# Stick-breaking attention: items taken two by two in the order of work

## The reference

```python
def stick_breaking_block(q_blk, k_ctx, v_ctx, q0):
    ...
    z = jnp.einsum('bthd,bshd->bhts', q_blk, k_ctx) * (SB_HEAD_DIM ** -0.5)
    before = jnp.arange(s_len)[None, :] < (q0 + jnp.arange(tq))[:, None]
    log_keep = jnp.where(before, jax.nn.log_sigmoid(-z), 0.0)
    csum = jnp.cumsum(log_keep, axis=-1)
    weights = jnp.where(before, jnp.exp(jax.nn.log_sigmoid(z) + csum[..., -1:] - csum), 0.0)
    return jnp.einsum('bhts,bshd->bthd', weights, v_ctx)

def stick_breaking_layer(h, norm_w, w_in, w_out):
    u = rmsnorm(h, norm_w)
    q, k, v, g = jnp.split(u @ w_in, 4, axis=-1)
    ...
    o = (o * jax.nn.silu(g.astype(jnp.float32))).astype(h.dtype)
    return h + o @ w_out
```

## Time and profile before

| | |
|---|---|
| runs, us | 3859.55, 3864.09, 3866.41 (median 3864.09) |
| span of the profiled execution | 3862.8 us |
| PE busy | 3735.6 us (97%) |
| DVE, ACT, POOL busy | 2372.8, 1653.3, 1689.3 us |

### The profile page before, as it was taken

The page is one execution under the profiler, slowest core; times in us unless marked ns, Lnnn a source line. Parts: engine busy times, 40 slices in busy tenths (PEclk is TensorE's granted clock), DMA queues, the critical chain, the costliest instruction groups (busy, mean ns, idle before and its releaser), DMA issues.

```text
span 3862.8 us, 50418 instructions
## 1 busy us (share of the span) xinstructions
PE 3735.6 (97%) x19892; PEld 3040.4 (79%) x19892; DVE 2372.8 (61%) x3104; ACT 1653.3 (43%) x2799; POOL 1689.3 (44%) x1108
## 2 busy tenths in 40 slices
PE   8999999999999899999999899999999999999998
PEld 6888887666655466888887799999878988888877
DVE  7667685633555548667684767554577156666664
ACT  5333444322222335333444553411572356666663
POOL 4555554344444535555553243422532233443464
PEclk9999999999999999999999999999999999999999
DMA  3234574200000121234574011221121300000024
GB/s 121 96 109 150 194 247 135 88 23 28 22 17 17 50 85 57 96 113 153 202 238 133 29 44 44 65 89 61 48 69 56 134 32 23 30 25 28 28 69 140
DMA packets 143917, 327.30 MB, mean 85 GB/s; under 512 B 16896, under 2 KB 20512, under 8 KB 143296
## 3 DMA queue, kind: packets, MB, share of 16 engines
q1 hardware_dynamic: 132368, 281.80, 21.9%
q0 software_dynamic: 8752, 39.65, 2.7%
q10 hardware_dynamic: 2560, 2.61, 0.2%
HBM read 252.37 MB, written 71.63 MB: 84 GB/s over the span
## 4 chain that ended last, share of the span: by engine, by line
PE 78%; DVE 13%; ACT 5%; POOL 2%; issue 2%; DMA 0%; ACTq 0%; DVEq 0%; SPq 0%; POOLq 0%
PE ps L958 6%; PE ps L959 6%; PE ps L960 6%; PE ps L414 5%; PE ps L415 5%; PE ps L416 5%; PE ps L4316 4%; PE ps L978 3%; PE ps L977 3%; PE ps L976 3%; PE ps L4248 2%; PE ps L4250 2%; PE ps L4249 2%; PE ps L2059 2%; PE ps L4300 2%; PE ps L2061 2%
## 5 line engine op out<-in xcount | busy, mean ns | idle before, releaser
L388 POOL TENSOR_TENSOR wlo<-raw,whi 128x1024 fp32r<-128x1024 f32 x154 | 377.1, 2453 | 483.9 <-ACT whi L379 483.7
L414 PE MATMUL ps<-xh,whi 128*128 128x352 f32 (+1 forms) x1400 | 473.3, 338 | 7.4 <-DVE xl L671 2.7
L415 PE MATMUL ps<-xh,wlo 128*128 128x352 f32 (+1 forms) x1400 | 450.6, 322 | 0.0
L416 PE MATMUL ps<-xl,whi 128*128 128x352 f32 (+1 forms) x1400 | 450.1, 321 | 0.0
L861 POOL TENSOR_TENSOR fwl<-fpb,fwh 128x512 fp32r<-128x512 f32 x204 | 302.3, 1491 | 267.1 <-ACT fwh L851 266.8
L861 POOL TENSOR_TENSOR fwl<-fpa,fwh 128x512 fp32r<-128x512 f32 x202 | 293.6, 1462 | 278.9 <-ACT fwh L851 278.8
L4621 POOL TENSOR_TENSOR ospl<-osp,osph 128x672 fp32r<-128x672 f32 (+4 forms) x144 | 190.9, 1326 | 357.9 <-ACT osph L4442 356.8
L414 PEld LDWEIGHTS ps<-xh,whi 128*128 128x128 f32 x1400 | 265.4, 190 | 19.2 <-POOL wlo L388 6.6
L415 PEld LDWEIGHTS ps<-xh,wlo 128*128 128x128 f32 x1400 | 264.3, 189 | 8.0 <-issue 2.2
L416 PEld LDWEIGHTS ps<-xl,whi 128*128 128x128 f32 x1400 | 264.1, 189 | 0.0
L958 PE MATMUL ps<-fxh,fwh 128*128 128x512 f32 x640 | 249.3, 390 | 1.3 <-ACT u L1036 1.3
(11 more groups left out here) (505 smaller groups left out, 9708.4 us busy)
## 6 DMA issues: line engine op xcount, KB each, us to landing
raw<-in_w_dram SPq DMA_DIRECT2D x154, 512.0 KB, 3.7
hs_scratch<-u SPq DMA_DIRECT2D x176, 256.0 KB, 2.4
u<-hs_scratch SPq DMA_DIRECT2D x118, 256.0 KB, 2.9
fpa<-in_fg_dram SPq DMA_DIRECT2D x88, 256.0 KB, 3.8
fpb<-in_fg_dram SPq DMA_DIRECT2D x88, 256.0 KB, 3.8
fpa<-in_fd_dram SPq DMA_DIRECT2D x88, 256.0 KB, 3.5
fpb<-in_fd_dram SPq DMA_DIRECT2D x88, 256.0 KB, 3.7
acc<-hs_scratch SPq DMA_DIRECT2D x80, 256.0 KB, 2.7
```

Of the source, the lines that this page charges most:

```text
L388: pool.x.tensor_tensor(K.wlo[n % 3][:, :], K.raw[n % 2][:, :], K.whi[n % 3][:, :], ALU.subtract).then_inc(*S.up("w_lo", n))
L414: pe.x.matmul(out, wh, xh, start=k == 0, stop=False)
L415: pe.x.matmul(out, wl, xh, start=False, stop=False)
L416: last = pe.x.matmul(out, wh, xl, start=False, stop=k == K - 1)
```

## The change

Items are taken in steps of two, (0, 1), (2, 3) and so on; nine steps for each head pair. In a step with items a' and b' the list has, in this order: if the first of the two items from two steps ago was the last of its chunk, its mix; z of a' and z of b'; a turn; the remaining mixes of two steps ago; then, once for a' and once for b': its copy, the sums of one of the previous step's items (a, then b), four fill steps, that item's rest, and the soft of a' (or b'). The splitting of weights by POOL (lo unit) and the issue of gate loads come at the end of a step. The places of the last pair's extra work are set anew, and its fill begins after eight items, where it began after six. No instruction's shape and no buffer is altered.

```diff
--- before.py
+++ after.py
@@ -4131,28 +4131,26 @@
 
 def _odd_places():
 
-    out, pipe = [], [None] * 5
-
-    def step(it, lo_unit):
-        pipe.insert(0, it)
-        if pipe[1]:
-            out.append(("soft", pipe[1]))
+    out, pipe = [], [(), (), ()]
+
+    def step(items, lo_unit):
+        pipe.insert(0, items)
+        first = int(len(pipe[2]) > 0 and pipe[2][0][3] == 0)
+        out.extend(("mix", it) for it in pipe[2][:first])
+        out.extend(("z", it) for it in items)
+        for it in items:
+            if it[1] < 7 and it[0] % PER_T in (12, 14, 16):
+                out.append(("turn", (it[1] + 1, it[0] % PER_T // 2 - 6)))
+        out.extend(("mix", it) for it in pipe[2][first:])
+        for m in range(2):
+            out.extend(("copy", it) for it in items[m:m + 1])
+            out.extend(("sums", it) for it in pipe[1][m:m + 1])
+            out.append(("fill", 4))
+            out.extend(("rest", it) for it in pipe[1][m:m + 1] if it[3])
+            out.extend(("soft", it) for it in items[m:m + 1])
         if lo_unit is not None:
             out.append(("lo unit", lo_unit))
-        if it is not None:
-            out.append(("z", it))
-            if it[1] < 7 and it[0] % PER_T in (12, 14, 16):
-                out.append(("turn", (it[1] + 1, it[0] % PER_T // 2 - 6)))
-            out.append(("copy", it))
-        if pipe[3]:
-            out.append(("mix", pipe[3]))
-        if pipe[2]:
-            out.append(("sums", pipe[2]))
-        out.append(("fill", 4))
-        if pipe[2] and pipe[2][3]:
-            out.append(("rest", pipe[2]))
-        if pipe[4] and not pipe[4][3]:
-            out.append(("gate", 3 * pipe[4][1] + pipe[4][2] + 2))
+        out.extend(("gate", 3 * it[1] + it[2] + 2) for it in pipe[2] if not it[3])
         pipe.pop()
 
     unit = UNIT_AT["Q.8"] + 3
@@ -4160,35 +4158,34 @@
         if t < 7:
             out.append(("begin", t + 1))
         lo_unit = None
-        for m, it in enumerate(ODD[PER_T * t:PER_T * (t + 1)], 1):
-            step(it, lo_unit)
+        for m in range(0, PER_T, 2):
+            step(ODD[PER_T * t + m:PER_T * t + m + 2], lo_unit)
             lo_unit = None
-            if t < 7 and m % 6 == 2:
+            if t < 7 and m % 6 == 0:
                 unit += 1
                 lo_unit = unit
                 out.append(("hi unit", unit))
             if t == 7:
-                out.extend(LAST_PAIR.get(m, ()))
+                out.extend(LAST_PAIR[m // 2])
         if t < 7:
             out.append(("fill", 1000))
-    for _ in range(4):
-        step(None, None)
+    for _ in range(2):
+        step((), None)
     out.extend([("fill", 1000), ("part", (2, 4)), ("rows", (2, 0)), ("rows", (2, 1))])
     return out
 
 
-LAST_PAIR = {m: [("part", (0, m - 1))] for m in (1, 2, 3, 4)}
-LAST_PAIR[5] = [("part", (1, 0))]
-LAST_PAIR[6] = [("part", (0, 4)), ("begin", 8)]
-LAST_PAIR[4].append(("rows", (0, 0)))
-LAST_PAIR[7] = [("rows", (0, 1)), ("part", (1, 1))]
-LAST_PAIR[8] = [("part", (1, 2))]
-LAST_PAIR[9] = [("rows", (1, 0)), ("part", (1, 3))]
-LAST_PAIR[10] = [("part", (2, 0))]
-LAST_PAIR[11] = [("part", (2, 1))]
-LAST_PAIR[12] = [("part", (1, 4))]
-LAST_PAIR[13] = [("rows", (1, 1)), ("part", (2, 2))]
-LAST_PAIR[14] = [("part", (2, 3))]
+LAST_PAIR = {
+    0: [("part", (0, 0)), ("part", (0, 1))],
+    1: [("part", (0, 2)), ("part", (0, 3)), ("rows", (0, 0))],
+    2: [("part", (1, 0))],
+    3: [("part", (0, 4)), ("begin", 8), ("rows", (0, 1)), ("part", (1, 1))],
+    4: [("part", (1, 2))],
+    5: [("rows", (1, 0)), ("part", (1, 3)), ("part", (2, 0))],
+    6: [("part", (1, 4)), ("part", (2, 1))],
+    7: [("rows", (1, 1)), ("part", (2, 2))],
+    8: [("part", (2, 3))],
+}
 ODD_PLACES = _odd_places()
```

## The result

| | before | changed |
|---|---|---|
| median of four runs each, us | 3864.6 | 3898.98 |
| range of the runs | 3859.55 to 3866.41 | 3892.84 to 3901.18 |
| span of the profiled execution | 3862.8 | 3891.0 |

The changed kernel is slower: the ratio is 1.0086, with a 95% interval from 1.0071 to 1.0101. (The kernel before has one run more here than in the table ahead of the prediction.) The profiled execution was the quickest of its four (3892.84); the others had spans of 3896.4 to 3899.3 at a mean clock of 0.983, against 0.985 in the profiled one.

The account below looks back on a forecast made before the run. PE, busy 97% of the span, was taken as the bound. Per pair -2.8 + 4.2 + 3.0 - 0.6 = +3.8 us, 26.6 in seven, and -2.5 for the last pair gave span 3886.9, time 3887.5; 8-in-10 range 3858 to 3907.

Parts of the forecast that it names:

- The saving: PE's matmuls in each head pair: fewer changes of array shape save 2.8 us per pair, bounds 2.4 and 3.3.
- The first wait: z of a step's second item waits for the max of the previous step's second item: 4.2 us per pair.
- The second wait: Second item's min waits for POOL ahead of turn's copy, copy and add, so PE waits: 3.0 us per pair net.
- The overlap: Pairs 0 to 6: a PE that comes later waits less at four places, so 0.6 us per pair comes off.
- The last pair: Last head pair, with eight items without fill in place of six: taken as -2.5 us, from -6 to +6.
- A: Rival: faster, only the saved shape switches count and the waits of z and min don't bind; 3842 us, chance 0.20.
- B: Rival: no change, z waits as computed but the min doesn't hold back copy and add; 3866.5 us, chance 0.15.
- C: Rival: slower still, both waits lengthen each other, each step loses 0.2 us more; 3904 us, chance 0.15.

Follow-up runs that it names:

- e3_both: Changed kernel with the max of each step's second item ahead of the second fill and its min behind the first item's add; 3840.07 us, ratio 0.9931.
- e8_ctrl: Kernel before, items single, with the max of every item ahead of the fill; 3863.32 us, ratio 1.0000.
- e2_min: Changed kernel with min, exp and ln of each step's second item moved behind the add of the previous step's first item; 3869.01 us, ratio 1.0009.
- e1: Changed kernel with DVE taking the max of each step's second item ahead of the second fill, and so of the low part; 3854.94 us, ratio 0.9969.
- e6: Kernel before with z of the odd item drawn up behind z of the even one, all else single; 3882.58 us, ratio 1.0050.
- e4_last: Changed kernel with the last pair's fill beginning after six items, as before, in place of eight; 3887.89 us, ratio 1.0056.
- e7_all: Changed kernel with second item's max ahead of the second fill, its min behind the add, and last pair's fill from item 6; 3835.38 us, ratio 0.9925.

## Why the prediction was right, and where its terms were off

The direction was right, and the time of 3887.5 lies 11.5 us under the median, in the range. Against its own execution the sum gave a span of 3886.9 where 3891.0 came. That is two errors that partly cancel: pairs 0 to 6 gave +23.0 at the last gate multiply of pair 6 (3690.31 before, 3713.27 now) where the sum had +26.6, and the tail gave +5.3 where the sum had -2.5. Together they are 28.3, the whole difference of the spans (28.2). That the sum missed the span by 4.1 only is thus in part luck. The other 7.4 of the 11.5 us lie outside the sum. 6.1 are those by which the median is above the profiled execution. The rest is what lies around the span: 1.8 in that execution, where the forecast allowed 0.6 (3886.9 with the 1.3 that it names would have been 3888.2). Of the longer executions no trace exists, and their lower mean clock (0.983) only suggests that the last pair's slow stretch was longer in them.

**The saving, -2.8.** PE has the same order in e3_both as in the changed kernel, so e3_both is what the waits are measured against. It gives 3.3 a pair for the switches (above), of which up to 0.15 may be the early max, by what e8_ctrl gained beside the turn's wait. The term was 0.5 too small, at the upper end of its bounds (2.4 and 3.3). That a second z pays no change of shape holds where no mask lies between; here the second z of a chunk of values, PE in the changed kernel:

```profile
3484.35 0.32 PE L4297 MATMUL ps<-oql,okh 64*128 64x352 f32 x2
3484.51 0.17 PE L4297 MATMUL ps<-oqh,okh 64*128 64x16 f32 x2
...
3484.98 1.08 PE L4343 MATMUL ps<-oz,ovt 128*64 128x192 f32 x8
```

The two z stand 0.16 apart, as the prediction said.

**The first wait, +4.2.** Measured, by how much later than in e3_both a z starts behind the matmul ahead of it: 0.89, 0.77, 0.64 and 0.81 for z of items 15, 17, 1 and 3, then 0.22 for 5 and none for 7, so 3.3. The prediction had for the same six 0.98, 0.87, 0.84, 0.98, 0.38 and 0.15, each too long by 0.09 to 0.20. Half or more of that is one number: from DVE's end to PE's start I took 0.15, from the turn's copy, and here it is 0.05 (3511.76 to 3511.81), 0.1 in each wait. Against it stands a cost that the prediction did not have: behind a wait the next two matmuls of z come late too. In the changed kernel, and at the same place in e3_both, where z does not wait:

```profile
3511.81 0.42 PE L4297 MATMUL ps<-oqh,okh 64*128 64x336 f32 x2 [0.73 <-DVE osp L4537]
3512.07 0.32 PE L4297 MATMUL ps<-oqh,okl 64*128 64x336 f32 x2
```

```profile
3483.66 0.32 PE L4304 MATMUL ps<-oqh,okh 64*128 64x336 f32 x2
3483.82 0.32 PE L4304 MATMUL ps<-oqh,okl 64*128 64x336 f32 x2
```

That is 0.26 where 0.16 passes without a wait, the same 0.1 that the earlier trace rows has behind a change of shape. Two of the z waits pay it, so the first wait costs 3.5 in all; e2_min and e3_both, which differ by this wait, are 3.5 apart. The mechanism was right, and e1 and e6 show it from either side. The seven pairs have 35 such waits by starts, of which the view lists 27, not 42.

**The second wait, +3.0 net.** Measured by starts, each against the usual distance: 1.22 (step 14, 15), 0.73 (16, 17), 1.20 (6, 7) and 0.50 (12, 13), together 3.65 where the prediction had 1.16, 0.73, 1.24 and 0.55, together 3.68. Of the last, 0.2 stays in e3_both. Behind three of these waits, too, the next matmul is late by 0.1. So what the min costs is 3.8, as e2_min says, less 0.6 that the turns of before lost beyond e3_both: 3.2 net. The min waits for POOL in the whole layer as foretold; DVE's waits, pairs 0 to 6 of the changed kernel:

```profile
DVE osp L4521 <- POOL ospl L4618: 64.9, 41, 2.3
```

e2_min, which takes this wait away, got 3.8 back.

**The overlap, -0.6.** The sum for a pair, with the measured terms, is -3.3 + 3.5 + 3.8 - 0.6 = +3.4, which is what was measured, and leaves nothing for an overlap. The term stood for a path that my adding up left 1.3 us short, and no run shows it. With a first wait that was 0.7 too large and a saving and a second wait that were 0.5 and 0.2 too small, it brought the total within 0.4 of what was measured; so near a sum is luck, the signs and the order of the terms are not.

**The last pair, -2.5: the term that was mis-sized.** It measured +5.3 over the tail (+6.8 from the end of pair 6's projection, just outside its own bound of +6). The step that failed is the sentence that the waits of the bare items "run beside each other": it gave two more items without fill no price, with the reason that 64 fill steps are there in either kernel. But PE can't fill its waits in a bare item, and here it also ran at the lower of the clock's two levels. The first row matmul came at 3742.03 where it came at 3707.24. PE in the changed kernel, two bare items:

```profile
3732.44 0.74 PE L4313 MATMUL ps<-osph,orest 128*128 128x192 f32 x2 [0.74 <-DVE oz L4545]
3732.98 0.63 PE L4313 MATMUL ps<-ospl,orest 128*128 128x192 f32 x2
3733.41 0.79 PE L4313 MATMUL ps<-osph,ontri 128*128 128x320 f32 x2
3733.99 0.73 PE L4313 MATMUL ps<-ospl,ontri 128*128 128x320 f32 x2
3735.64 0.90 PE L4313 MATMUL ps<-osph,orest 128*128 128x320 f32 x2 [0.92 <-DVE oz L4545]
```

Matmul pairs of 320 columns start 0.58 to 0.70 us apart, where at the full clock they start 0.29 apart (3483.25 and 3483.54, pair 4), and the rest of each item waits 0.7 to 0.9 us for the add. Before, the last pair had the lower clock for two stretches:

```profile
3690.80:3701.00 10.20, 9.17 (x44) 6.84 (x46) 4.06 (x10) 5.54 (x12) 7.72 (x8) 0.50 0.25 77
3704.50:3711.30 6.80, 6.80 (x32) 6.26 (x32) 3.87 (x5) 5.07 (x9) 4.82 (x5) 0.50 0.00 0
```

That is 17.0 us against 27.3. Ten more microseconds at the lower level, with PE busy 89% of them (24.29 of 27.30), would cost about 10.3 x 0.89 / 2 = 4.6 us, an estimate from these rows. e4_last removes 10.2 of the 10.3 and 5.2 of the 5.3, but there both went with the two items. e1_max speaks for a smaller share of the clock. It has the eight bare items too, and the lower level for 17.1 us, no longer than the kernel before; its last pair:

```profile
3666.00:3764.30 98.30, 87.73 (x558) 70.50 (x557) 54.74 (x86) 64.56 (x101) 70.01 (x52) 0.91 0.23 76
```

Its tail of 88.0 is still 3.0 above that of before, and 2.3 below the changed kernel's. So at an equal time at the lower level more than half of the loss remains, and that is waiting. The parting is not clean: e1_max moves the max in the last pair as well, and e8_ctrl, which moves it with single items and has 17.1 us at the lower level, has a tail 1.1 longer than before. The price could have been read ahead: the mean clock of 0.54 in the earlier trace rows was the row, and I used it only to say that the bare items were slow already.

**The rivals.** A falls by e1 and the pair of 85.0; B by e2. C, whose 3904 lies nearer the median, has a pair of 87.2, and the narrow steps show no waits that it needs: between items 8 and 12 PE waits for nothing. That the median came close to it is due to the last pair, and to executions longer than the profiled one. The Trainium skill says in "TensorEngine Tiling (Array Packing)", Key Properties, that a change of tiling mode drains TensorE, and that alone would have given A. The runs agree that fewer changes save time, 3.3 us a pair, and e3_both's 3840.07 is near A's 3842; but that does not decide until the order frees PE of the two waits.

## What to carry to other kernels

Putting two units of work side by side on the bound engine asks for each of its inputs half a step earlier: look for every hand-over behind it that has buffers for two units only (here the banks that the max frees, and the osp buffers that POOL frees), and take care of its place in the helpers' order with the same edit: here the max went ahead, and the min that waits went back. The order on the helpers was worth 7.4 us a pair here, the joined matmuls 3.3. And price the edges of a pipeline, where there is no filler, apart: two more items without cover cost 5.3 us there, as much as the change cost in one and a half pairs.

## What the runs showed of the hardware that I had not expected

- How long the lower clock lasts. With eight bare items in the last pair the changed kernel had a granted clock of 0.50 for 27.3 us in one piece, and e2_min too; but e1_max had it for 3.4, 3.4 and 10.2 us, e3_both for 13.7, and e7_all, with six bare items, for 6.8. In the changed kernel it fell after five waits of PE of 0.56 to 1.35 us, and it rose again while row matmuls ran without a break. The kernels with the first of the two waits taken away had it for less time; what exactly tips it, these runs do not settle.
- From the end of DVE's max to the start of the waiting z there are 0.05 us, and from the end of the turn's copy to the waiting projection 0.06 (3515.81 to 3515.87); the 0.15 of the earlier trace rows is not the price of a hand-over in general. At the first turn of a pair it is 0.15 in the changed kernel too; why there, these runs do not show.
- A wait of PE costs more than the wait. The next pair of matmuls behind the pair that waited starts 0.26 us after it in place of 0.16 (3511.81 and 3512.07), where both have the same shape and 336 columns. So the 0.105 that the prediction read behind a change of shape in the earlier trace rows comes behind a wait as well.
- A joined pair of mixes saves 0.19 us by starts, about the 0.195 of entering z alone.
